# A new order for the beginning of a hybrid S5 / convolution trunk: inputs by quarters, the u projection one parameter group later, powers and copies moved between engines

## The chip, the cores and the metric

The kernel runs on one core of one Trainium2 chip. The metric is the device time of one execution in microseconds (us); the time before is the median of three executions, 2514.39 us (2512.59 to 2515.88).

## The reference

One inference step of two layers over a prompt of 1024 tokens and 8 sample tokens, d = 1024, in float32. Every layer is modulated by a shift, a scale and a gate that come from a conditioning vector (9 columns: one of the prompt, eight of the samples). Only the beginning matters here:

```python
mods = (silu(c) @ w_ada + b_ada).reshape(n, DEPTH, 2, 3, D)      # 96 blocks of 128 outputs
shift, scale, gate = mods[:, i, 0, 0], mods[:, i, 0, 1], mods[:, i, 0, 2]
h = x * (1.0 + scale) + shift
u = h @ w_in                                                     # then S5, 64 groups, 64 states
a_bar = exp(lam * dt); b_bar = ((a_bar - 1.0) / lam) * b
# states by a scan over time: s = a_bar * s + b_bar u;  y = re(c s) + d_skip * u
```

Behind it come the GLU of the S5 layer, a layer norm, a convolutional FFN, the short-convolution layer and a second FFN.

## The kernel before

Five engines run hand-written programs that meet at semaphores. Features lie on partitions: x is 8 chunks (k) of 128 features by 1032 tokens. A product in float32 is made of three float32r products: WH x HH, WH x HL, WL x HH, where HH and HL are the high and low half of the activations and WH and WL those of a weight unit (128 x 1024). `up_half` (L602) computes a part of one third (344 tokens) of one unit; a unit has three thirds of 8 x 3 matmuls.

**Loads.** One SyncE queue (L321) loads the conditioning vector, constants, then all eight first adaLN pairs (`FIRST`, 1 MB each; a pair is two of the 96 blocks), two raw units of w_in, the x chunks, and the other constants. Further adaLN pairs are loaded into the two slots of `ADA` from ScalarE's queue (`load_pair`, L1080), each when the pair two before has been multiplied (`take_partial`, L1085).

**First modulation.** TensorE multiplies the first eight pairs (L624), transposes their results (L632), Vector adds the bias (L1562), ScalarE modulates x chunk by chunk into a scratch tile (L1103), Vector makes HH by a cast and HL by a subtraction (L1566). The first product of u waits for all of it (`s_xfree`, L705), and for four more adaLN pairs.

**Eight groups.** For n = 0 to 7 TensorE computes one unit of u with three adaLN pairs between its parts (L707), then `s5_input(n)` (L645, transposes W2) and `s5_param(n)` (L654, the K0 products and the transposed B). Of a pair, `ada_partial` multiplies, ScalarE copies out, `ada_sum` adds the four partial sums, and ScalarE writes them to MOD (`take_mod`, L1092).

**Vector** computes the discretization (L1504 to L1538), the powers of a_bar in AP_ one by one (L1546), nine squarings of the unit angle factor, the last seven of them in UP7 (L1549 to L1557), eight copies into AR, the modulation above, then BB, and for each group `s5_params` (L1613): W2, the output constants CA, small copies into BD and CD, the rotation tables (which need the factor tables TA and TB16, `s_rtab`), and the K0 copy. Results go through SyncE to memory (L362) in one store of WT, CA, BD, CD, one of the rotation and one of K0.

**GpSimd** writes both halves of the weight units (`split_unit`, L452) and builds TA and TB16 by doubling (`factors`, L461; scratch in RB). It starts when the eighth first pair has been multiplied (L450), and the tables when `s_u7` says that the powers are ready.

Behind the last group follow the chunked scan (from `chunk_inputs(0)`, L820) and all later stages.

## Time and profile before

| | us |
|---|---|
| median of three executions | 2514.39 |
| the profiled execution | 2515.28 |
| its span in the profile | 2513.5 |
| TensorE busy | 2407.2 (96%) |
| VectorE busy | 1653.5 (66%) |
| ScalarE busy | 645.4 (26%) |
| GpSimd busy | 1015.3 (40%) |

The profile is of one execution. Times count from the start of its span. PE is TensorE's matmuls, PEld its weight loads, DVE VectorE, ACT ScalarE, POOL GpSimd, SP SyncE; a letter q behind an engine is its queue. L12 is line 12 of the kernel. In a timeline row stand start, duration, engine, line, instruction, output<-inputs with shapes and count, and in brackets how long the engine was idle before and what released it. Matmuls overlap, so their rate is read from the distance of their starts. The granted clock is a share of TensorE's full 2.4 GHz; 0.50 is 1.2 GHz.

### The profile page before, as it was taken

What the parts mean: (1) busy time and instruction counts of PE and PEld (TensorE: products, weight loads), DVE (VectorE), ACT (ScalarE), POOL (GpSimd) and SP (SyncE); (2) the same over time, 40 slices, a digit from 0 to 9 for tenths busy, and PEclk for the clock granted to TensorE, in tenths of its full rate; (3) what the DMA queues carried; (4) which work ended last, traced back from release to release, by engine and by line L of the source; (5) the groups of instructions that cost most, each with busy time, mean ns of one, the idle gap of its engine ahead of it and who ended that gap; (6) DMA issues with size and microseconds to landing.
All of it is one profiled execution on the core that took longest, in us unless ns stands there. A gap on an engine that the chain in (4) does not pass through costs nothing.

```text
span 2513.5 us, 39721 instructions
## 1 busy us (share of the span) xinstructions
PE 2407.2 (96%) x16080; PEld 2292.2 (91%) x16080; DVE 1653.5 (66%) x2230; ACT 645.4 (26%) x1273; POOL 1015.3 (40%) x505
## 2 busy tenths in 40 slices
PE   5898989999999999999999999999999999999996
PEld 2787789989999999999988999998999999999994
DVE  7888853367766666666774553575766676666675
ACT  1223421154212222222234101115222221221223
POOL 3322024347444434444325533434644443434430
PEclk8899999999999999999999999999999999999997
DMA  8686941111111111111101111110111111111102
GB/s 311 245 300 220 323 169 59 43 34 43 51 51 43 43 43 51 51 51 43 51 26 48 59 51 43 51 34 26 59 51 43 51 43 51 43 51 44 43 25 76
DMA packets 78112, 197.18 MB, mean 78 GB/s; under 512 B 27264, under 2 KB 34944, under 8 KB 76928
## 3 DMA queue, kind: packets, MB, share of 16 engines
q1 hardware_dynamic: 60992, 152.03, 17.7%
q10 hardware_dynamic: 16960, 42.80, 4.8%
q8 instruction: 127, 2.08, 0.3%
q14 instruction: 33, 0.27, 0.0%
HBM read 175.57 MB, written 19.23 MB: 78 GB/s over the span
## 4 chain that ended last, share of the span: by engine, by line
PE 81%; DVE 8%; ACT 4%; DVEq 3%; DMA 2%; issue 2%; SPq 0%; ACTq 0%
PE bank L609 17%; PE bank L611 17%; PE bank L610 17%; PE bank L886 8%; PE bank L888 7%; PE bank L887 7%; PE bank L589 1%; DVEq L2006 1%; PE bank L875 1%; PE bank L877 1%; PE bank L876 1%; DVE ROWS L2004 1%; PE bank L928 1%; ACT HH L1288 1%; ACT XRAW L1278 1%
## 5 line engine op out<-in xcount | busy, mean ns | idle before, releaser
L455 POOL TENSOR_TENSOR WH<-RAW,ZERO 128x1024 fp32r<-128x1024 f32 x188 | 389.9, 2074 | 1327.8 <-PE bank L611 632.9
L609 PE MATMUL bank<-HH,WH 128*128 128x344 f32 x2856 | 919.8, 322 | 1.1 <-ACT MOD L1097 0.7
L610 PE MATMUL bank<-HL,WH 128*128 128x344 f32 x2856 | 913.1, 320 | 0.0
L611 PE MATMUL bank<-HH,WL 128*128 128x344 f32 x2856 | 913.0, 320 | 0.0
L609 PEld LDWEIGHTS bank<-HH,WH 128*128 128x128 f32 x2856 | 537.2, 188 | 11.4 <-issue 11.4
L611 PEld LDWEIGHTS bank<-HH,WL 128*128 128x128 f32 x2856 | 537.5, 188 | 0.0
L610 PEld LDWEIGHTS bank<-HL,WH 128*128 128x128 f32 x2856 | 537.4, 188 | 0.0
L457 POOL TENSOR_TENSOR WL<-RAW,WH 128x1024 fp32r<-128x1024 f32 x188 | 530.6, 2822 | 14.7
L1847 DVE SCALAR_TENSOR_TENSOR X<-bank,MOD,X 128x344 f32<-128x344 f32 (+1 forms) x480 | 273.8, 571 | 325.6 <-PE bank L888 241.3
L886 PE MATMUL bank<-GH,WH 128*128 128x344 f32 x1248 | 408.3, 327 | 10.6 <-DVE X L1871 8.1
L888 PE MATMUL bank<-GH,WL 128*128 128x344 f32 x1248 | 399.6, 320 | 0.0
L887 PE MATMUL bank<-GL,WH 128*128 128x344 f32 x1248 | 399.4, 320 | 0.0
L886 PEld LDWEIGHTS bank<-GH,WH 128*128 128x128 f32 x1248 | 234.1, 188 | 30.4 <-DVE X L1871 11.0
L887 PEld LDWEIGHTS bank<-GL,WH 128*128 128x128 f32 x1248 | 234.8, 188 | 0.9
L888 PEld LDWEIGHTS bank<-GH,WL 128*128 128x128 f32 x1248 | 234.5, 188 | 0.0
L2004 DVE SCALAR_TENSOR_TENSOR ROWS<-ROWS,CWF 128x1024 f32<-128x1024 f32 x84 | 186.2, 2217 | 53.3 <-ACT ROWS L1346 53.3
L1367 ACT ACTIVATE ROWS<-ROWS 128x1032 f32<-128x1032 f32 x42 | 44.9, 1070 | 637.7 <-DVE ROWS L2010 637.7
L1346 ACT ACTIVATE ROWS<-bank,CWF 128x344 f32<-128x344 f32 x252 | 167.9, 666 | 0.0
L1342 ACT ACTIVATE ROWS<-bank 128x344 f32<-128x344 f32 (+1 forms) x252 | 119.1, 473 | 121.5 <-PE bank L611 108.1
L875 PE MATMUL bank<-HH,WH 128*128 128x344 f32 x384 | 129.0, 336 | 14.4 <-issue 11.5
L2009 DVE SCALAR_TENSOR_TENSOR ROWS<-STF,CWF,ROWS 128x8 f32<-128x8 f32 x84 | 131.1, 1561 | 13.6 <-issue 12.3
L2005 DVE SCALAR_TENSOR_TENSOR ROWS<-STF,CWF,ROWS 128x8 f32<-128x8 f32 x84 | 130.7, 1555 | 0.0
(329 smaller groups left out, 2434.6 us busy)
## 6 DMA issues: line engine op xcount, KB each, us to landing
RAW<-in_wstream SPq DMA_DIRECT2D x188, 512.0 KB, 3.2
ADA<-in_wada ACTq DMA_DIRECT2D x40, 1024.0 KB, 6.0
s_pack<-PKA SPq DMA_DIRECT2D x7, 1344.0 KB, 6.3
PKA<-s_pack SPq DMA_DIRECT2D x10, 512.0 KB, 6.8
XRAW<-in_xT SPq DMA_DIRECT2D x8, 516.0 KB, 16.5
X<-in_xT SPq DMA_DIRECT2D x1, 4128.0 KB, 12.3
PKA<-s_pack SPq DMA_DIRECT2D x7, 576.0 KB, 5.0
...
```

The source lines that it names most:

```text
L455: pool.tensor_tensor(WH[:, slot, :], RAW[:, slot % 2, :], bc(ZERO[:, :], [128, 1024]), ALU.add).then_inc(s_hi, 1)
L457: pool.tensor_tensor(WL[:, slot, :], RAW[:, slot % 2, :], WH[:, slot, :].bitcast(F32), ALU.subtract)\
L609: pe.matmul(o, wh, hh, start=k == 0, stop=False)
L610: pe.matmul(o, wh, hl, start=False, stop=False)
L611: m = pe.matmul(o, wl, hh, start=False, stop=k == KC - 1)
L875: pe.matmul(o, wh, hh, start=k == 0, stop=False)
L886: pe.matmul(out, wh, gh, start=q == 0, stop=False)
L887: pe.matmul(out, wh, gl, start=False, stop=False)
L888: m = pe.matmul(out, wl, gh, start=False, stop=q == 1)
L1346: act.activation(Tr[:, TH * t:TH * (t + 1)], b[:, 0:TH], ACT.Identity, bias=cwr[:, bass.ds(row, 1), 3:4].rearrange("p a b -> p (a b)"), sc ...
L1847: stt(xo, b[:, 0:w], MOD[:, gsec + o, 0:1], xo, M, A).then_inc(s_dev, 1)
L2004: stt(Tr[:, 0:SEQ], Ur[:, 1:1 + SEQ], cw[1], Tr[:, 0:SEQ], M, A)
```

## The change

The first loads are reordered: for each of four quarters p a shift pair, its scale pair, two x chunks, and for p < 2 a raw unit; then constants, and the first two pairs of `ADA` from SyncE's queue. The first pairs are multiplied with the packed form that the later pairs already use (`first_partial`, `first_sum`), ScalarE writes their modulations, then HH directly and the modulated chunk in place; Vector only subtracts (`chunks_low`). `first_u(p)` computes a quarter of the contraction (two chunks) of units 0 and 1 into six banks. The groups then hold units 2 to 7: group 0 has no u, and the others `U_STEP` thirds and `P_STEP` pairs each, pairs alternating between banks 4 and 5, thirds going through banks 0 to 3. Before, 4 later pairs stood ahead of u and 24 in the groups; now all 28 stand in the groups. The powers of a_bar are computed by doubling (three products of 32, 64 and 128 columns). The nine angle squarings and the modulation of the samples (`samples`, five small operations with four drains) are GpSimd's. ScalarE writes the high halves of units 0 to 9 (`hi_unit`) and the copies into BD and CD; GpSimd writes their low halves (`low_unit`, as `split_unit` without its first operation). Vector's group is split: W2 of group j, K0 of group j - 1, rotation j (rotation 0 only in group 1), output constants of group j. The store of a group is split in two, and `s5_param` now waits also for `s_ca`, the output constants.

```diff
+U_STEP = (0, 3, 3, 2, 2, 3, 2, 3)
+P_STEP = (2, 3, 3, 4, 4, 3, 5, 4)
+U_BANK = (0, 1, 2, 3, 0, 1, 2, 3, 0, 1, 2, 3, 0, 1, 2, 0, 1, 0)
+U_FREE = (0, 0, 0, 0, 1, 2, 3, 4, 5, 6, 7, 8, 9, 10, 11, 13, 14, 16)
+HI_AFTER = {1: 4, 2: 5, 3: 6, 5: 7, 6: 8}
...
-for i in range(8):
-    sp.dma_start(FIRST[i], wada[2 * i:2 * i + 2, :, :].rearrange("a p n -> p a n")).then_inc(s_first[i], 16)
-for n in range(2):
-    sp.dma_start(RAW[:, n, :], wstream[S_ORD[n], :, :]).then_inc(s_raw[n], 16)
-for k in range(KC):
-    sp.dma_start(XRAW[:, k, :], xT[:, k, :]).then_inc(s_xin[k], 16)
+for p in range(4):
+    for f, u in ((2 * p, 2 * p), (2 * p + 1, 8 + 2 * p)):
+        sp.dma_start(FIRST[f], wada[u:u + 2, :, :].rearrange("a p n -> p a n")).then_inc(s_first[f], 16)
+    for k in range(2 * p, 2 * p + 2):
+        sp.dma_start(XRAW[:, k, :], xT[:, k, :]).then_inc(s_xin[k], 16)
+    if p == 2:
+        for i in range(2):
+            sp.dma_start(BR[:, i], bT[i]).then_inc(s_br, 16)
+    if p < 2:
+        sp.dma_start(RAW[:, p, :], wstream[S_ORD[p], :, :]).then_inc(s_raw[p], 16)
...
+sp.wait_ge(s_fprod, 2)
+for a in range(2):
+    sp.dma_start(ADA[:, a], wada[ADA0 + 2 * a:ADA0 + 2 * a + 2, :, :].rearrange("a p n -> p a n"))\
+        .then_inc(s_adain[a], 16)
...
+def store_outputs(j):
+    sp.wait_ge(s_bdtev, j + 1)
+    sp.wait_ge(s_ca, j + 1)
+    sp.wait_ge(s_cd, j + 1)
+    sp.dma_start(pack_dram[j, :, PK_CA:PK_ROT], PKA[:, PK_CA:PK_ROT]).then_inc(s_pkc, 16)
+def store_k0(j):
     sp.wait_ge(s_kr, j + 1)
     sp.dma_start(k0_dram[j], KR).then_inc(s_krd, 16)
+for j in range(KC):
+    if j:
+        store_outputs(j - 1)
+        store_k0(j - 1)
     if j < KC - 1:
         sp.wait_ge(s_wtev, 2 * (j + 1))
-        sp.wait_ge(s_bdtev, j + 1)
-        sp.wait_ge(s_bd, j + 1)
-        sp.dma_start(pack_dram[j, :, 0:PK_ROT], PKA[:, 0:PK_ROT]).then_inc(s_pk, 16)
+        sp.dma_start(pack_dram[j, :, 0:PK_CA], PKA[:, 0:PK_CA]).then_inc(s_pkw, 16)
+        for i in ((), (0, 1))[j] if j < 2 else (j,):
+            sp.wait_ge(s_rot6, i + 1)
+            sp.dma_start(pack_dram[i, :, PK_ROT:PK], RB[i % 2]).then_inc(s_pkr[i % 2], 16)
     if j < 6:
         load_unit(j + 4, j % 2, S_ORD[j + 4] - j - 4 if j < 4 else 0)
-sp.wait_ge(s_pk, 16 * (KC - 1))
+store_k0(KC - 1)
+sp.wait_ge(s_pkw, 16 * (KC - 1))
+sp.wait_ge(s_pkc, 16 * (KC - 1))
 for i in range(2):
     sp.wait_ge(s_pkr[i], 64 - 16 * i)
...
+def angle_power(i):
+    z = [RB[1][:, 512 + NP_ * k:512 + NP_ * (k + 1)] for k in range(4)]
...
+    up = lambda lv: (UP7[:, 0, lv, :], UP7[:, 1, lv, :])
+    src = (Q[:, 17, :], Q[:, 18, :]) if i == 0 else z[2 * i - 2:2 * i] if i < 3 else up(i - 3)
+    product(z[2 * i:2 * i + 2] if i < 2 else up(i - 2), src, src, v)
...
-for n in range(2):
-    split_unit(n, n)
+for p in range(2):
+    low_unit(p, p)
+    samples(p)
+pool.wait_ge(s_fprod, 4)
 pool.wait_ge(s_u7, 1)
+for i in range(9):
+    if i == 4:
+        samples(2)
+    angle_power(i)
+samples(3)
+for n in range(2, 4):
+    low_unit(n, n % 2)
 factors(TB16, 0, 4)
 factors(TA, 4, 3).then_inc(s_rtab, 1)
-for n in range(2, U_S5):
-    pool.wait_ge(s_up, 3 * (n - 1))
-    split_unit(n, n % 2)
-pool.wait_ge(s_up, 3 * (U_S5 - 1))
-split_unit(U_S5, 0)
+for n in range(4, U_S5):
+    low_unit(n, n % 2)
+low_unit(U_S5, 0)
 pool.wait_ge(s_rot6, KC)
 pool.wait_ge(s_bdt, KC)
 pool.memset(TT[:, :, :], 0.0).then_inc(s_ones, 1)
 pool.wait_ge(s_krd, 16 * KC)
...
+def first_u(p):
+    pe.wait_ge(s_xfree, 2 * (p + 1))
+    for n in range(2):
+        pe.wait_ge(s_unit, n + 1)
+        for t in range(3):
+            if t == 2:
+                pe.wait_ge(s_xsmp, p + 1)
+            m = up_half(n, t, 2 * p, 2 * p + 2)
+            if p == 3:
+                m.then_inc(s_up, 1)
+pe.wait_ge(s_silu, 2)
+for p in range(4):
+    first_partial(2 * p)
+    first_partial(2 * p + 1)
+    if p == 0:
+        pe.wait_ge(s_cst, 16 * N_CST)
+    first_sum(2 * p)
+    first_sum(2 * p + 1)
+    if p > 1:
+        first_u(p - 2)
+first_u(2)
+first_u(3)
 pe.wait_ge(s_ones, 1)
...
+def pair(a):
+    if a:
+        ada_sum(a - 1, BK[4 + (a - 1) % 2][:, 256:274])
+    if a > 1:
+        pe.wait_ge(s_mod, a - 1)
+    ada_partial(a, BK[4 + a % 2][:, 0:256])
...
+    end = a + P_STEP[n]
+    if not U_STEP[n]:
+        pair(a)
+        a += 1
+        s5_input(n)
+    for i in range(U_STEP[n]):
+        if i == 1:
+            pe.wait_ge(s_kr, n)
+            pe.wait_ge(s_bdtev, n)
+            s5_input(n)
+            if n == KC - 1:
+                to_tokens(0)
+        pe.wait_ge(s_unit, 2 + m // 3 + 1)
+        if m > 3:
+            pe.wait_ge(s_ev, 6 + U_FREE[m])
+        third_of_u(m, 0, 4)
+        pair(a)
+        third_of_u(m, 4, 8).then_inc(s_up, 1)
+        m, a = m + 1, a + 1
     if n == KC - 1:
         to_chunks(0)
-    up_half(slot, 2, 2, 6)
-    ada_sum(a + 2, BK[6][:, 0:18])
-    if n == KC - 1:
-        pe.wait_ge(s_mod, a + 3)
-        s5_input(n)
-    up_half(slot, 2, 6, 8).then_inc(s_up, 1)
-    if n < KC - 1:
-        pe.wait_ge(s_mod, a + 3)
-        s5_input(n)
+    while a < end:
+        pair(a)
+        a += 1
     s5_param(n)
+ada_sum(a - 1, BK[4 + (a - 1) % 2][:, 256:274])
...
+def hi_unit(n):
+    slot = n % 2
+    if n > 1:
+        act.wait_ge(s_up, 3 * (n - 1))
+    act.wait_ge(s_raw[slot], 8 * (n - slot) + 16)
+    act.activation(WH[:, slot, :], RAW[:, slot, :], ACT.Copy).then_inc(s_hi, 1)
...
+        act.activation(LC[:, 0, k:k + 1], BK[7][:, 256 + 9 * i:257 + 9 * i], ACT.Identity, bias=LC[:, 1, k:k + 1])
...
+    for k in range(2 * p, 2 * p + 2):
+        act.wait_ge(s_xin[k], 16)
+        xk = XRAW[:, k, 0:SEQ]
+        act.activation(HH[:, k, 0:SEQ], xk, ACT.Identity, bias=MOD[:, k, 0:1], scale=LC[:, 0, k:k + 1])
+        act.activation(xk, xk, ACT.Identity, bias=MOD[:, k, 0:1], scale=LC[:, 0, k:k + 1]).then_inc(s_hx, 1)
+    if p < 2:
+        hi_unit(p)
...
+def take_bd(j):
     act.wait_ge(s_bdt, j + 1)
     act.activation(PKA[:, PK_BD:PK_BD + 256], BK[7][:, 0:256], ACT.Copy).then_inc(s_bdtev, 1)
...
+def b_diagonal(j):
+    if j:
+        act.wait_ge(s_k0, j)
...
+        for pl in range(2):
+            m = act.activation(BD[rows, pl, :, g2, :], BB[rows, pl, 4 * j:4 * j + 4, :], ACT.Copy)
+    m.then_inc(s_bd, 1)
...
+for n in range(2):
+    for t in range(3):
+        take_third(n, t)
+    hi_unit(2 + n)
...
+        take_bd(n - 1)
+    b_diagonal(n)
+    if not U_STEP[n]:
+        take_pair(a)
+        a += 1
+        take_input(n)
+    for i in range(U_STEP[n]):
+        if i == 1:
+            take_input(n)
+            if n == KC - 1:
+                act.wait_ge(s_pkr[1], 48)
+                take_tokens(0)
+        take_pair(a)
+        take_third(2 + m // 3, m % 3)
+        m, a = m + 1, a + 1
+    if n == KC - 1:
+        act.wait_ge(s_pkr[0], 64)
+        take_chunks(0)
+    sample_outputs(n)
+    while a < end:
+        take_pair(a)
+        a += 1
+    if n in HI_AFTER:
+        hi_unit(HI_AFTER[n])
+take_bd(KC - 1)
+take_mod(a - 1, BK[4 + (a - 1) % 2][:, 256:274])
+hi_unit(U_S5 + 1)
...
+def chunks_low(p):
+    for k in range(2 * p, 2 * p + 2):
+        dve.wait_ge(s_hx, k + 1)
+        tt(HL[:, k, 0:SEQ], XRAW[:, k, 0:SEQ], HH[:, k, 0:SEQ].bitcast(F32), S_).then_inc(s_xfree, 1)
...
-for k in range(2, KPH):
-    cmul((ap(0, k), ap(1, k)), (ap(0, k - 1), ap(1, k - 1)), (ap(0, 1), ap(1, 1)), tmp4)
...
+chunks_low(0)
+for m in (1, 2, 4):
...
+    cmul([AP_[:, pl, :, m + 1:2 * m + 1] for pl in range(2)],
+         [AP_[:, pl, :, 1:m + 1] for pl in range(2)], base, w)
+chunks_low(1)
...
 for k in range(L):
-    m = dve.tensor_copy(AR[:, :, :, L - 1 - k], AP_[:, :, :, k])
-m.then_inc(s_u7, 1)
...
 for j in range(KC):
-    s5_params(j, j == 0)
+    s5_input(j)
+    if j:
+        s5_kernel(j - 1)
+        if j == 1:
+            s5_rotation(0)
+        s5_rotation(j)
+    s5_outputs(j)
+s5_kernel(KC - 1)
```

## Rows read from the trace of the kernel before

**Rows 1.** The page's first part: busy microseconds and share of each engine.

```profile
PE 2407.2 (96%) x16080; PEld 2292.2 (91%) x16080; DVE 1653.5 (66%) x2230; ACT 645.4 (26%) x1273; POOL 1015.3 (40%) x505
```

**Rows 2.** Windows: length, busy us (count) by engine, clock, DMA share, GB/s.

```profile
10.00:40.00 30.00, 29.79 (x142) 12.68 (x140) 23.88 (x158) 2.35 (x4) 1.22 (x1) 1.00 1.03 408
72.00:97.00 25.00, 22.83 (x172) 19.18 (x172) 23.39 (x45) 5.59 (x17) 8.64 (x11) 0.88 0.46 167
97.00:230.10 133.10, 128.66 (x1110) 108.50 (x1110) 108.47 (x199) 37.93 (x108) 27.57 (x12) 0.99 0.81 294
98.00:100.00 2.00, 1.48 (x16) 0.69 (x16) 1.83 (x6) 0.00 (x0) 0.00 (x0) 0.58 0.55 217
114.26:132.86 18.60, 18.20 (x160) 15.39 (x158) 16.17 (x30) 5.18 (x15) 5.29 (x2) 1.00 0.84 301
47.57:76.20 28.63, 14.74 (x91) 9.27 (x92) 22.82 (x37) 12.47 (x20) 26.51 (x46) 0.50 0.68 239
```

**Rows 3.** TensorE's timeline: start, duration, instruction, idle before and releaser.

```profile
8.91 3.57 PE L627 MATMUL bank<-ADA,SC 128*9 128x256 f32 x8 [8.91 <-DMA ADA<-in_wada]
...
56.00 1.93 PE L589 MATMUL bank<-ADA,SCP 128*32 128x256 f32 x16 [16.21 <-DMA ADA<-in_wada]
58.95 0.99 PE L598 MATMUL bank<-STK,EVA 128*128 128x9 f32 x4 [1.01 <-ACT EVA L1090]
...
73.06 0.62 PE L609 MATMUL bank<-HH,WH 128*128 128x344 f32 x1 [0.71 <-ACT MOD L1097]
...
102.04 0.32 PE L609 MATMUL bank<-HH,WH 128*128 128x344 f32 x1
102.20 0.32 PE L610 MATMUL bank<-HL,WH 128*128 128x344 f32 x1
...
114.26 1.03 PE L650 MATMUL bank<-IDN,BR 128*128 128x128 f32 x8
115.70 0.67 PE L660 MATMUL bank<-PKA,BD 128*32 128x128 f32 x16 [0.40 <-ACT PKA L1163]
...
116.49 0.40 PE L609 MATMUL bank<-HH,WH 128*128 128x344 f32 x1
...
229.77 0.44 PE L666 MATMUL bank<-IDN,BD 128*128 128x128 f32 x2
```

**Rows 4.** Vector's timeline, 38 to 106 us.

```profile
38.64 8.87 DVE L1559 COPY AR<-AP_ 128x64 f32<-128x64 f32 x8
...
92.33 2.23 DVE L1671 TENSOR_TENSOR TP<-AW 128x512 f32<-128x512 f32 x1
...
98.51 0.69 DVE L1621 TENSOR_TENSOR TP<-AR,BB 128x512 f32<-128x512 f32 x1
...
102.01 0.69 DVE L1629 TENSOR_TENSOR BR<-TP 128x512 f32<-128x512 f32 x1
105.34 0.76 DVE L1640 TENSOR_TENSOR TP<-AP_,CR 128x576 f32<-128x576 f32 x1 [2.64 <-DMA s_pack<-PKA]
```

**Rows 5.** ScalarE's timeline at the first modulation.

```profile
49.02 2.37 ACT L1107 ACTIVATE UALL<-XRAW,MOD,LC 128x1024 f32<-128x1024 f32 x2 [9.69 <-issue]
```

**Rows 6.** GpSimd's timeline, 40 to 76 us.

```profile
40.82 2.34 POOL L457 TENSOR_TENSOR WL<-RAW,WH 128x1024 fp32r<-128x1024 f32 x1
...
47.93 0.26 POOL L470 TENSOR_TENSOR AW<-AW,UP 128x32 f32<-128x32 f32 x1
...
49.60 0.31 POOL L470 TENSOR_TENSOR AW<-AW,UP 128x64 f32<-128x64 f32 x1
...
63.98 0.62 POOL L473 TENSOR_TENSOR AW<-AW,UP 128x256 f32<-128x256 f32 x1
...
75.29 0.91 POOL L476 TENSOR_TENSOR AW<-AW 128x128 f32<-128x128 f32 x1
```

**Rows 7.** Instructions on tile ADA, 0 to 230 us: its loads' time to landing.

```profile
DMA to landing us min/median/max: 4.7/5.6/10.0
```

More of the change, by code:

```diff
@@ L52 @@
 NG = (96 - ADA0) // 2
-G_X, G_U = 4, 3
+G_U = sum(P_STEP)
 G_SCAN = (2, 2, 2, 2, 2, 1, 1)
@@ new lines, in first_sum @@
+            def first_sum(f):
+                pe.wait_ge(s_fev, f + 1)
+                for i in range(2):
+                    m = pe.matmul(BK[6 + f % 2][:, 256 + 9 * i:256 + 9 * (i + 1)], EVA[:, f % 2, 128 * i:128 * (i + 1)],
+                                  STK[:, :], start=True, stop=True, skip_group_check=True)
+                m.then_inc(s_ftr, 1)
+            def first_u(p):
[8 more added lines that the diff above has]
+                            m.then_inc(s_up, 1)
@@ new lines, in pair, with third_of_u @@
+            def pair(a):
[4 more added lines that the diff above has]
+                ada_partial(a, BK[4 + a % 2][:, 0:256])
+            def third_of_u(m, k0, k1):
+                n, t = 2 + m // 3, m % 3
+                o = BK[U_BANK[m]][:, 0:TH]
+                for k in range(k0, k1):
+                    wh = WH[:, n % 2, 128 * k:128 * (k + 1)]
+                    wl = WL[:, n % 2, 128 * k:128 * (k + 1)]
+                    hh, hl = HH[:, k, TH * t:TH * (t + 1)], HL[:, k, TH * t:TH * (t + 1)]
+                    pe.matmul(o, wh, hh, start=k == 0, stop=False)
+                    pe.matmul(o, wh, hl, start=False, stop=False)
+                    last = pe.matmul(o, wl, hh, start=False, stop=k == KC - 1)
+                return last
@@ new lines, in b_diagonal, with sample_outputs @@
+            def b_diagonal(j):
+                if j:
+                    act.wait_ge(s_k0, j)
+                else:
+                    act.wait_ge(s_pw, 1)
+                for g2 in range(2):
+                    rows = slice(64 * g2, 64 * (g2 + 1))
+                    for pl in range(2):
+                        m = act.activation(BD[rows, pl, :, g2, :], BB[rows, pl, 4 * j:4 * j + 4, :], ACT.Copy)
+                m.then_inc(s_bd, 1)
+            def sample_outputs(j):
+                if j:
+                    act.wait_ge(s_pkc, 16 * j)
+                else:
+                    act.wait_ge(s_cst2, 16 * N_CST2)
+                CD = PKA[:, PK_CD:PK_CD + 256].rearrange("p (x a b c) -> p x a b c", x=2, a=4, b=2)
+                for g2 in range(2):
+                    rows = slice(64 * g2, 64 * (g2 + 1))
+                    for pl in range(2):
+                        m = act.activation(CD[rows, pl, :, g2, :], CR[rows, pl, 4 * j:4 * j + 4, :], ACT.Copy,
+                                           scale=float(1 - 2 * pl))
+                m.then_inc(s_cd, 1)
@@ L1618, in s5_params @@
                 fence()
-                if not first:
+                if j:
                     dve.wait_ge(s_wt, 2 * j)
@@ L1635, in s5_params @@
                 fence()
-                if not first:
-                    dve.wait_ge(s_pk, 16 * j)
-                    dve.wait_ge(s_k0, j)
+                if j:
+                    dve.wait_ge(s_pkc, 16 * j)
                     dve.wait_ge(s_bdt, j)
@@ L1674, in s5_params, with s5_kernel @@
                 tt(R[:, 1], t[0], t[1], A).then_inc(s_rot6, 1)
+            def s5_kernel(j):
                 dve.wait_ge(s_k0, j + 1)
-                if not first:
+                if j:
                     dve.wait_ge(s_krd, 16 * j)
```

287 lines of the change are left out of this document (122 added, 165 removed).

## The prediction, made before the changed kernel ran

> **What bounds the kernel now.** I read the page first, then the windows of the beginning, then the timelines engine by engine. TensorE is busy 96% of the span [rows 1], so only its holes or its work can give time. The change touches nothing behind the point where the last parameter group is done, 230.1 us into the span (the last of [rows 3]); from there on both kernels run the same code on the same waits, so I forecast that point and move the rest of the span with it.
>
> Up to there three stages. First, 10 to 40 us: the queue moves 408 GB/s at a DMA share of 1.03 [rows 2]; it is full, and everything needed waits for it: the 8 MB of the first eight adaLN pairs are loaded before x. The first pair is there at 8.9 us [rows 3]. Second, 40 to 73 us: TensorE hardly works. Its next pair is waited for until 56.0 us, four pairs follow one by one, and the first product of u starts at 73.1 us [rows 3]. Vector's chain of powers and copies stands ahead of the modulation (the eight copies into AR alone end at 47.5 us) [rows 4]. Third, 73 to 230 us: eight groups, each one unit of u (3 thirds of 24 matmuls), three adaLN pairs and one S5 parameter group. One takes 18.60 us, of which TensorE is busy 18.20, at a clock of 1.00 and a DMA share of 0.84 (301 GB/s) [rows 2]. Here TensorE bounds, and Vector with 16.17 us follows closely.
>
> **Prices.** A matmul of 344 columns starts 0.157 us after the one before it (102.04 and 102.20 in [rows 3]), a third of u is 3.8 us. Transposes and products of one S5 group take 114.26 to 116.49 = 2.2 us, 0.4 of it a wait [rows 3]. So a pair with its sum and its restarts costs (18.6 - 72 x 0.157 - 2.2)/3 = 1.7 us. On Vector, W2 of one group is 98.51 to 102.70 = 4.2 us, the output constants are six operations of 0.76 us with the same two fences, 4.6 us [rows 4]; the rotation has six of W2's size, 4.2 us; with the K0 copies 0.5 us, a group is 13.5 us. On ScalarE a modulation of one x chunk is 1.2 us [rows 5]. On GpSimd a low half is 2.34 us; a complex product of 32 columns takes 47.93 to 49.60 = 1.67 us, its multiply of 256 columns 0.62 us undisturbed [rows 6]. The levels of the two factor tables are then 1.7, 2.0, 2.6, 3.9 and 1.7, 2.0, 2.6 us (the middle ones interpolated), with memsets about 17.5 us; in this trace they took 47.6 to 76.2 us, 28.6, while Vector was busy 22.8 us beside them [rows 2, 6].
>
> **Part 1, a new order of loads and u in quarters.** Pairs arrive as shift, scale, two x chunks, a raw unit. Counting megabytes behind the first landing at 0.41 MB/us: the scale pairs land at 11.5, 20.4, 29.4 and 38.4 us, the last x chunk at 41. From a landed pair to its modulation is partial 1.9, copy, sum 1.0, scalar copies (56.0 to 59.9 in [rows 3]), about 4.5 us at half clock. ScalarE then works 4 x 1.2 = 4.8 us for two chunks (high half and the chunk itself), where before Vector cast; the four quarters are ready at about 20, 30, 39 and, because the first quarter of u stands ahead of the last pairs on TensorE, not 47 but 51 us. Vector subtracts (1.2 us each). A quarter of the first two units is 36 matmuls, 5.7 us at full clock, about 8 at first (after the 2.6 us hole before 98.5 the clock granted was 0.58 in 98 to 100 us [rows 2]). Laid end to end: 33.5 to 41.5, two pairs, 45 to 62 us for three quarters. So two units are done at 62 us, where before the second ended at 114. Removed from the path: 23 us of waiting with TensorE idle or at 1.2 GHz.
>
> **Part 2, angle powers and samples to GpSimd.** Nine products of 1.67 us = 15 us and three of the four sample steps (five small operations and four drains, by the same row 2 us each) stand behind the second low half, which ends at 33.5 us: 54.5 us undisturbed. Vector works beside most of it, in operations of 0.7 to 1.2 us, so I take 60. The last samples are needed at 58.4, so TensorE loses 2 us. Less than nothing it can't cost, since the modulation never waited for these samples alone; the other end is rival (c). Low halves 2 and 3 wait for ScalarE, which waits for units 0 and 1: 68 us. Then the tables: 17.5 undisturbed, 28.6 as before; Vector has little to do after 70 us, so I take 19.5: 88 us.
>
> **Part 3, a new wait.** Vector does not ask for the tables in group 0 any more, but in group 1, ahead of the output constants of group 1. From 70 to 88 us it stands still. Then rotations 0 and 1 and the constants: 4.2 + 4.2 + 4.6 = 13.0 us, 101 us. Low half 4 will hold a Vector operation as now (a multiply of 0.69 us took 2.23 [rows 4]); this is inside my rounding of 3 us. TensorE, from 64, has group 0 (two pairs, no u) and group 1 (three thirds, three pairs), 5 + 17.5 us, is through at 86 and waits some 14 us for the constants of group 1. The eight small copies into BD and CD leave Vector for ScalarE, 1 us a group; ScalarE is busy 5.2 of 18.6 us [rows 2], so this costs and gains nothing.
>
> **Part 4, six groups from 101 us on.** 15 thirds, 23 pairs, 6 S5 groups without the 0.4 wait, tokens and chunks 2.1: 15 x 3.8 + 23 x 1.6 (one restart fewer, since sum and partial now stand together) + 6 x 1.8 + 2.1 = 107 us. Added: half clock after the wait, 2.5. Pairs with no u beside them: the load of a pair goes out when the pair two before is done, and takes 5.6 us to land [rows 7], so the second such pair waits 2.5 us and the group with three of them 3.3; with the copy between partial and sum in such a place (0.6 us at this clock), three groups, 8 us. High half 6 on ScalarE waits for a third that TensorE computes only in the next group; behind it on ScalarE are the copy of the transposed B, the next pair's copy and its load: 2 us at the B copy, 1 for the load behind it. Vector with 13.5 us a group and one hold of 1.5 stays inside the 17 to 20 of TensorE. Sum 107 + 2.5 + 8 + 3 = 120. By bytes: 23 pairs of 1.05 MB, six sets of stores of 1.97 and four raw units of 0.52 are 38 MB, at 301/0.84 = 358 GB/s 106 us, so the queue is close behind, but not the bound. So the last group ends at 101 + 120 = 221, say 220 us against 230.1: **10 us less**. The profiled execution took 2515.3 us with a span of 2513.5; it stood 0.9 above the median 2514.4. 2515.3 - 10 = 2505.3; against the median 2504.4; I say 2505.
>
> **Rivals.** (a) *The shared work hardly collides and loads keep up*: tables at 82 us, constants at 95, six groups in 109 us: 204, gain 26 us, 2489. For it: the six groups' matmuls fill only 107 us. Against: the DMA share of 0.84 at an 18.6 us group. (b) *The gain is given back at the ceilings*: DMA at 1.0 delays each pair by another microsecond, and the tables come at 92: constants at 106, 124 us behind them: 230, no change, 2515. For it: 28.6 us for tables of 17.5. (c) *Slower*: GpSimd and Vector run one after another. From 33.5 us on Vector has at most 28 us of work before the samples end; if all of it stands ahead of GpSimd's 21 us, the last samples are there at 83, two units at 87, low halves 92, tables 110, constants 123, groups 120: 243, 13 us slower, 2528. It decides from where the tables are later than 103 us. Against it: in 47.6 to 76.2 us Vector was busy 22.8 us [rows 2] and GpSimd, with 17.5 us of its own, ended 12 us earlier than the sum of both. The Trainium skill ("SBUF — State Buffer", Who interferes with whom) states this as a rule: a Vector instruction with two SBUF inputs and a GpSimd instruction that reads SBUF exclude each other for a whole instruction, and the loser blocks. By that rule in full, (c) would be the forecast, 2528. The trace agrees with holds of single instructions (0.69 became 2.23), not with full serial running. (d) *The change does not do what it says*: a quarter is held by another engine, so u starts late; with the first two units at 75 instead of 62 the tables and all behind move 13 us: (b)'s time or up to 2518.
>
> **Chances.** Forecast with its near surroundings (2498 to 2509) 0.50, (a) 0.20, (b) and (d) 0.20, (c) 0.10. For 8 in 10 the range leaves out (c) and the far end of (a): 2489 to 2516. About 0.2% (5 us) is what a measurement can tell from no change; so faster 0.70, same 0.20, slower 0.10. The likeliest case is faster, 2498 to 2509.
>
> **What would show it.** Units 0 and 1 done near 62 us (ScalarE's sixth copy of u); modulated x chunks in pairs 9 us apart; nine complex products on GpSimd between 34 and 60 us; the tables' end at 88 us; a wait of TensorE of 14 us for Vector's constants of group 1, with half clock behind it; then groups of 16 to 22 us with waits of 2 to 3 us for adaLN loads where no u is beside them, and a DMA share near 0.95; everything behind the last group shifted by one constant. I am wrong if GpSimd ends the tables outside 82 to 100 us, if Vector rather than TensorE sets the six groups, or if the stages after them do not shift alike.

## The result, and the profile of the changed kernel

The changed kernel takes 2527.28 us (median of 5 executions, 2524.47 to 2530.45), the kernel before 2514.64 on the same chip (5 executions, 2512.59 to 2516.0): a ratio of 1.005 with the interval 1.0036 to 1.0065. It is **slower by 12.6 us**; the forecast of 2505 was wrong in size and sign. The profile is of an execution of 2530.45 us, 3.2 above the median.

First the page: its busy times, which answer to [rows 1]. The work has hardly changed, the span has.

```profile
span 2528.7 us, 39804 instructions
PE 2398.7 (95%) x16096; PEld 2300.8 (91%) x16096; DVE 1616.9 (64%) x2075; ACT 680.9 (27%) x1383; POOL 1014.0 (40%) x569
```

Then windows, which answer to [rows 2] (length, then busy us and count by engine, clock, DMA share, GB/s): two stretches of the front, the stretch of the new wait, and the groups 2, 4 and 6 of the plan, counted from 0. A group is counted from the end of one block's last transposes of B to the end of the next block's.

```profile
50.00:60.00 10.00, 7.19 (x31) 7.19 (x32) 8.01 (x11) 0.00 (x0) 8.77 (x20) 0.66 0.03 13
60.00:70.00 10.00, 5.44 (x22) 5.16 (x22) 0.00 (x0) 2.84 (x5) 4.83 (x20) 0.74 0.00 1
100.00:120.00 20.00, 8.52 (x65) 7.54 (x66) 18.66 (x27) 2.45 (x10) 2.52 (x1) 0.66 0.40 141
113.20:132.40 19.20, 19.20 (x161) 16.95 (x160) 15.24 (x26) 6.44 (x23) 0.00 (x0) 0.93 0.76 265
151.10:176.70 25.60, 18.34 (x156) 14.90 (x155) 12.77 (x21) 7.63 (x27) 2.38 (x1) 0.83 0.73 264
194.90:221.60 26.70, 19.78 (x175) 15.17 (x175) 14.94 (x22) 9.60 (x32) 2.37 (x1) 0.81 0.75 274
```

In 50 to 70 us the queue moves next to nothing (0.03, 0.00) and the clock is between its two levels: TensorE has holes in the very stretch that was to be its best. In the six groups together (113.20 to 242.60 us) the DMA share is 0.77, where the prediction expected near 0.95. Groups 4 and 6 take 25.6 and 26.7 us for 18.3 and 19.8 us of matmuls; group 2, with the same kind of work, takes 19.2.

TensorE's waits of over 1.2 us in 48 to 222 us, from its timeline (start, duration, instruction, idle before and releaser), which answer to [rows 3]; two more waits for pair loads, of 2.26 us at 88.22 and 2.08 us at 148.88, are left out:

```profile
52.81 0.65 PE L677 MATMUL bank<-HH,WH 128*128 128x344 f32 x1 [4.01 <-POOL HL L508]
65.65 0.66 PE L677 MATMUL bank<-HH,WH 128*128 128x344 f32 x1 [4.56 <-POOL HL L508]
...
111.48 1.10 PE L754 MATMUL bank<-PKA,BD 128*32 128x128 f32 x16 [13.25 <-issue]
...
159.10 1.06 PE L743 MATMUL bank<-IDN,BR 128*128 128x128 f32 x8 [1.46 <-issue]
173.24 1.94 PE L657 MATMUL bank<-ADA,SCP 128*32 128x256 f32 x16 [4.87 <-DMA ADA<-in_wada]
...
210.73 0.61 PE L666 MATMUL bank<-STK,EVA 128*128 128x9 f32 x4 [2.97 <-ACT EVA L1226]
214.38 1.93 PE L657 MATMUL bank<-ADA,SCP 128*32 128x256 f32 x16 [3.04 <-DMA ADA<-in_wada]
```

The first two are released by L508 on GpSimd, the low half of the eight sample columns. Each first matmul behind them lasts 0.65 us where one at full clock lasts 0.32: the engine comes back at 1.2 GHz. Units 0 and 1 are done at 72.4 us.

GpSimd's timeline there, which answers to [rows 6]:

```profile
39.07 0.26 POOL L518 TENSOR_TENSOR AW<-AW 128x32 f32<-128x32 f32 x1
39.47 1.30 POOL L512 TENSOR_TENSOR AW<-AW 128x32 f32<-128x32 f32 x1
40.73 1.22 POOL L513 TENSOR_TENSOR AW<-AW 128x32 f32<-128x32 f32 x1
...
52.27 0.48 POOL L508 TENSOR_TENSOR HL<-CB,HH 128x16 fp32r<-128x16 f32 x1
...
65.37 0.22 POOL L508 TENSOR_TENSOR HL<-CB,HH 128x16 fp32r<-128x16 f32 x1
69.38 2.37 POOL L490 TENSOR_TENSOR WL<-RAW,WH 128x1024 fp32r<-128x1024 f32 x1 [3.79 <-ACT WH L1185]
74.00 2.36 POOL L490 TENSOR_TENSOR WL<-RAW,WH 128x1024 fp32r<-128x1024 f32 x1 [2.24 <-ACT WH L1185]
76.30 0.15 POOL L532 MEMSET AW<- 128x32 f32 x1
...
95.42 0.46 POOL L518 TENSOR_TENSOR AW<-AW 128x128 f32<-128x128 f32 x1
```

The samples of quarter 2 end at 52.75, behind four angle powers, and those of quarter 3 at 65.59, behind all nine: TensorE starts again at 52.81 and 65.65. GpSimd then waits for ScalarE's copies, which wait for TensorE. The tables take 76.30 to 95.88 = 19.6 us. The 13.25 us of TensorE at 111.48 are the wait for the constants of the second group, which Vector can only begin behind tables and rotations (Vector idles 15.00 us up to 95.98 for `AW L518`).

The two long groups on ScalarE and SyncE's queue:

```profile
157.67 1.06 ACT L1185 ACTIVATE WH<-RAW 128x1024 fp32r<-128x1024 f32 x1 [6.86 <-PE bank L816]
157.70 0.37 ACTq L1218 DMA_DIRECT2D ADA<-in_wada  x1
158.63 0.37 ACT L1271 ACTIVATE PKA<-bank 128x256 f32<-128x256 f32 x1
...
198.73 0.33 SPq L354 DMA_DIRECT2D RAW<-in_wstream  x1
199.18 0.35 SPq L380 DMA_DIRECT2D s_pack<-PKA  x1
...
209.14 0.26 ACT L1301 ACTIVATE PKA<-CR 64x64 f32<-64x64 f32 x1 [2.23 <-DMA s_pack<-PKA]
```

In group 4 the high half of unit 6 (L1185, which waits for TensorE's third, `bank L816`) stands ahead of the copy of the transposed B (L1271), without which TensorE doesn't go on at 159.10. In group 6 the stores of block 5 (199.18) stand in SyncE's queue behind the load of unit 9 (198.73), which waits until GpSimd has done unit 7; ScalarE at L1301 and TensorE at 210.73 wait for these stores.

Behind the groups the shift is not constant. The last transposes end at 242.58, 12.4 us later than before (230.2, the last of [rows 3]; the prediction has 230.1), but the spans differ by 15.2 us. The K0 store behind them is issued at once and its readers start 4.4 us later, against 1.6 in the kernel before; two pair loads, issued at 237.49 and 241.80 by ScalarE's queue, are in front of it. The difference arises there: the products of L861, which wait for constants that the same queue reads back behind those readers, start at 255.86, 14.6 us later than before (241.22), after a wait of 7.41 us for 3.81; the transposes at 272.98 are 15.0 us late (257.96).

### The profile page after: what moved, and what is told of

Read it like the earlier page. It is cut to its first block, busy times and chain, and to the rows that moved or that the text cites. A ratio compares the mean times of both kernels' runs of the same rounds, so it can differ in the third digit from the quotient of the medians.

```text
span 2528.7 us, 39804 instructions
## 1 busy us (share of the span) xinstructions
PE 2398.7 (95%) x16096; PEld 2300.8 (91%) x16096; DVE 1616.9 (64%) x2075; ACT 680.9 (27%) x1383; POOL 1014.0 (40%) x569
## 3 DMA queue, kind: packets, MB, share of 16 engines
q8 instruction: 127, 2.08, 0.3%
## 4 chain that ended last, share of the span: by engine, by line
PE 80%; DVE 7%; ACT 3%; DVEq 3%; DMA 3%; issue 2%; POOL 1%; SPq 1%; POOLq 0%; ACTq 0%
PE bank L677 16%; PE bank L679 15%; PE bank L678 15%; PE bank L990 8%; PE bank L992 7%; PE bank L991 7%; DMA ADA<-in_wada 1%; PE bank L979 1%; DVEq L2174 1%; PE bank L981 1%; PE bank L980 1%; PE bank L657 1%; PE bank L814 1%; DVE ROWS L2172 1%; PE bank L815 1%
## 5 line engine op out<-in xcount | busy, mean ns | idle before, releaser
L677 PE MATMUL bank<-HH,WH 128*128 128x344 f32 x2712 | 870.1, 321 | 8.6 <-POOL HL L508 8.6
L678 PE MATMUL bank<-HL,WH 128*128 128x344 f32 x2712 | 868.4, 320 | 0.0
L679 PE MATMUL bank<-HH,WL 128*128 128x344 f32 x2712 | 868.2, 320 | 0.0
L480 POOL TENSOR_TENSOR WH<-RAW,ZERO 128x1024 fp32r<-128x1024 f32 x178 | 367.7, 2066 | 1196.2 <-PE bank L679 533.1
L677 PEld LDWEIGHTS bank<-HH,WH 128*128 128x128 f32 x2712 | 511.3, 189 | 9.1 <-POOL HL L508 9.1
L679 PEld LDWEIGHTS bank<-HH,WL 128*128 128x128 f32 x2712 | 511.6, 189 | 0.0
L482 POOL TENSOR_TENSOR WL<-RAW,WH 128x1024 fp32r<-128x1024 f32 x178 | 505.9, 2842 | 13.9
L678 PEld LDWEIGHTS bank<-HL,WH 128*128 128x128 f32 x2712 | 511.2, 188 | 0.0
L979 PE MATMUL bank<-HH,WH 128*128 128x344 f32 x384 | 129.9, 338 | 14.0 <-issue 11.5
## 6 DMA issues: line engine op xcount, KB each, us to landing
XRAW<-in_xT SPq DMA_DIRECT2D x8, 516.0 KB, 15.6
X<-in_xT SPq DMA_DIRECT2D x1, 4128.0 KB, 12.2
UALL<-in_wada SPq DMA_DIRECT2D x4, 1024.0 KB, 17.7
```

Source lines behind the costliest of these rows:

```text
L480: pool.tensor_tensor(WH[:, slot, :], RAW[:, slot % 2, :], bc(ZERO[:, :], [128, 1024]), ALU.add).then_inc(s_hi, 1)
L482: pool.tensor_tensor(WL[:, slot, :], RAW[:, slot % 2, :], WH[:, slot, :].bitcast(F32), ALU.subtract)\
L677: pe.matmul(o, wh, hh, start=k == 0, stop=False)
L678: pe.matmul(o, wh, hl, start=False, stop=False)
L679: m = pe.matmul(o, wl, hh, start=False, stop=k == KC - 1)
L979: pe.matmul(o, wh, hh, start=k == 0, stop=False)
```

## The experiments

Three theories came out of this. **A**: the order on GpSimd makes the front late. **D**: two order blocks lengthen groups 4 and 6; its rival **E**: the pair loads do. **B**: Vector and GpSimd slow each other, and the order has no weight, the near relation of the prediction's rival (c). A ratio is always to the kernel before on the same chip, with its 95% interval. Differences between two changed kernels are differences of medians; some were taken on different chips, where the kernel before had 2514.6, 2513.6, 2514.1 and 2512.8 us, so an error of 1 to 2 us must be allowed them. Ends of groups are from one profiled execution each. "Last group" is the end of the last transposes of B (230.2 before, 242.6 in the changed kernel), "tables" the end of the second table (95.9), "second group" the end of its transposes (113.2).

### The samples ahead of the powers

```diff
             for i in range(9):
-                if i == 4:
+                if i == 0:
                     samples(2)
+                if i == 4:
+                    samples(3)
                 angle_power(i)
-            samples(3)
```

> GpSimd takes the samples of unit 2 ahead of the first angle power and those of unit 3 ahead of the fifth, instead of behind the fourth and the ninth. Theory A (the order on GpSimd): TensorE loses its two waits for HL (4.01 us at 52.81 and 4.56 us at 65.65) and the stretches at 1.2 GHz behind them, so the high and low halves of units 0 and 1 are done at 60 to 62 us instead of 72. The powers still end at about 65.6, so the low halves of units 2 and 3 can follow at once and not at 69.4 and 74.0; the tables end at 89 to 91 instead of 95.9, the second rotation's constants at about 105 instead of 111.3, the time is 2520 to 2523. Theory B (Vector and GpSimd slow each other, and the order is of no weight): the tables keep their end near 96 whatever the samples' place, and the time stays at 2526 to 2529. Theory C (the whole loss lies in the group loop): the front may come earlier, but the groups stretch by as much, and the time stays at 2526 to 2529.

2520.63 us, 1.0037 (1.0023 to 1.0051): 6.6 us under the changed kernel. Windows of this kernel:

```profile
50.00:60.00 10.00, 10.00 (x65) 10.00 (x64) 8.81 (x12) 3.19 (x6) 8.63 (x19) 1.00 0.04 14
60.00:70.00 10.00, 5.16 (x67) 3.34 (x66) 4.48 (x8) 6.02 (x21) 9.09 (x20) 1.00 0.67 247
```

TensorE is busy 10.00 of 10 us at a clock of 1.00 where it had 7.19 at 0.66, and the queue, idle in 60 to 70 us before, is at 0.67. Tables 89.3, second group 106.5, last group 233.7. Theory A holds, as forecast here: units 0 and 1 are done at 60.3 us, and the six groups take 127.2 us for 129.4, so they don't stretch. B's and C's times did not come. The interval of the ratio still overlaps the changed kernel's (1.0036 to 1.0065), so it is the profile that shows the gain, not the time alone.

### The powers back on Vector

```diff
 # Vector, behind RHO
+            nine squarings of (q(17), q(18)) into UP7, then s_u7
 # GpSimd
-            wait s_u7; powers 0 to 3; samples(2); powers 4 to 8; samples(3)
+            samples(2); samples(3)
             for n in range(2, 4):
                 low_unit(n, n % 2)
+            pool.wait_ge(s_u7, 1)
             factors(TB16, 0, 4)
```

> The nine angle powers go back to Vector, between RHO and the AR copies; GpSimd does samples 2 and 3 at once, then the low halves of units 2 and 3, and then waits for the powers before the tables. Theory A (the order on GpSimd is what is late): units 0 and 1 are done on TensorE at 60 to 64, the tables end at about 87, the constants of the second rotation at about 102, and the time is 2517 to 2520, some 9 us under the changed kernel. Theory B (Vector and GpSimd slow each other): the same operations cost Vector more than the 10 to 12 us that they took off GpSimd, and the tables end at 92 or later, the time is 2523 or more. What is left over 2514.6 after this is the group loop's.

2523.03 us, 1.0031 (1.0018 to 1.0043). The tables end at 88.5 as expected, but the time is above the expected 2517 to 2520, in the range that was named for theory B, whose other signs (tables at 92 or later, the operations dearer on Vector) did not come. Two rows of this kernel, GpSimd and Vector:

```profile
61.21 2.56 POOL L490 TENSOR_TENSOR WL<-RAW,WH 128x1024 fp32r<-128x1024 f32 x1 [17.37 <-ACT WH L1182]
...
61.46 2.93 DVE L1806 TENSOR_TENSOR TP<-AP_,CR 128x576 f32<-128x576 f32 x1
64.46 2.77 DVE L1808 TENSOR_TENSOR PKA<-TP 128x576 f32<-128x576 f32 x1
```

On Vector the 54 operations take 35.12 to 43.90 = 8.8 us, where GpSimd needed 24. But GpSimd then stands idle for 17.37 us ahead of 61.21, with the powers ready at 44: the tables could have run there. A group loop left alone keeps its excess (last group 236.0, 130.4 us behind the second). Also, Vector's 0.76-us operations beside the low halves take 2.93 and 2.77.

### The high half of unit 6 one group later

```diff
-HI_AFTER = {1: 4, 2: 5, 3: 6, 5: 7, 6: 8}
+HI_AFTER = {1: 4, 2: 5, 4: 6, 5: 7, 6: 8}
```

> The high half of unit 6 is made in group 4 of the plan instead of group 3; nothing else moves. Theory D (an order block in the loop): in the changed kernel hi_unit(6) stands on ScalarE ahead of the copy of a pair's results that TensorE needs, and the fourth group took 25.5 us where its neighbours took 18.2 to 19. With the high half one group later that group takes 19 to 21 and the next gets at most 2 us longer; the last group ends at about 238 instead of 242.6 and the time is 2522 to 2524. Theory E (the group is long because adaLN pair loads come late, 4.87 us at 173.24): the group stays at 24 to 26 and the time at 2526 to 2529.

2521.88 us, 1.0030 (1.0012 to 1.0048). The group goes from 25.6 to 19.4 us, the next from 18.2 to 19.8, all six from 129.4 to 125.3; the last ends at 238.1. The copy that was held is that of the transposed B, not that of a pair's results. TensorE's wait for a pair load, and SyncE's queue, in this kernel:

```profile
167.83 1.93 PE L657 MATMUL bank<-ADA,SCP 128*32 128x256 f32 x16 [0.93 <-DMA ADA<-in_wada]
...
152.07 0.32 SPq L380 DMA_DIRECT2D s_pack<-PKA  x1
...
174.17 0.33 SPq L354 DMA_DIRECT2D RAW<-in_wstream  x1
```

The wait for a pair load falls from 4.87 to 0.93 us. SyncE's stores of the block wait for the same copy of B; in the changed kernel they went out at 159.02, in one bunch with the next stores and a raw unit (163.42), beside the pair load of 163.45, which took 9.8 us from its issue until TensorE could start (173.24); here they go out at 152.07, and the load of 162.00 takes 5.8. So the order block made the late load too: theory D for this group. The raw unit also goes out later here (174.17), and this run can't tell its share from that of the stores.

### Half of each later pair load

```diff
-                act.dma_start(ADA[:, a % 2], wada[ADA0 + 2 * a:ADA0 + 2 * a + 2, :, :]...)
+                act.dma_start(ADA[:, a % 2, 0], wada[ADA0 + 2 * a])
```

> Each later adaLN pair load brings only the first of its two blocks, so half of these bytes aren't moved; the values of the second block are left out of the computation (its buffer keeps what it had). Theory E (the pair loads bound the loop, as the queue is short of time there): the four waits of TensorE for ADA (12.2 us) go, with the half clock behind them; the groups from the second on take 18 to 19 each, the last ends at 230 or before, and the time is 2512 to 2518. The k0 store behind the last group lands 2 to 3 us sooner. Theory D (order blocks): the fourth and sixth group keep most of their excess of 7 us each, and the time falls by 3 to 5 us at most, to 2522 to 2525.

2513.93 us, 1.0002 (0.9993 to 1.0012). TensorE's waits in the first 280 us:

```profile
PE bank L754 <- issue: 16.6, 1, 16.6
PE bank L699 <- DMA ADA<-in_wada: 8.9, 2, 8.3
PE bank L677 <- POOL HL L508: 8.7, 2, 8.0
PE bank L861 <- DMA PKA<-s_pack: 5.8, 1, 5.8
...
PE bank L657 <- DMA ADA<-in_wada: 3.3, 3, 1.5
```

The waits of L657 were 12.2 us and are 3.3; the six groups take 118.1 us instead of 129.4, the last ends at 230.9, and the wait behind it (L861) is 5.8 instead of 9.9. The front is as late as in the changed kernel. So the loads' time is worth 11 us in the loop and some 2 behind it. Theory E's numbers came within 1 us, D's did not; but a load behind a bunch of stores is helped by half the bytes as well as by its stores going earlier, so this run doesn't refute D.

### A new order of the front

```diff
 # Vector: RHO; powers; chunks_low(2); AR and q; chunks_low(3); BB
 # GpSimd
+            samples(2)
+            samples(3)
             pool.wait_ge(s_u7, 1)
-            nine powers with the samples between and behind them
+            factors(TB16, 0, 4)
             for n in range(2, 4):
                 low_unit(n, n % 2)
-            factors(TB16, 0, 4)
             factors(TA, 4, 3).then_inc(s_rtab, 1)
```

> The angle powers on Vector directly behind RHO (54 operations that took 9.1 us there in the kernel a2), Vector's low halves 2 and 3 moved up behind them, and GpSimd in the order samples 2 and 3, first table, low halves of units 2 and 3, second table. In a2 GpSimd stood idle 17.37 us ahead of 61.21 although the powers were done at 44.0. The group loop is as in the changed kernel. Theory A (GpSimd's order sets the tables' end, and this sets TensorE's wait in the second group): tables done at 68 to 72 instead of 95.9, no wait of over 4 us of TensorE behind unit 2, the second transposes of BD at 88 to 92 instead of 113; the groups behind them become some us longer than 129 in all, because the loads have less time, the last ends at 222 to 228, the time is 2508 to 2513. Theory F (the group loop is bound by transfers, whatever its start): the last group ends where the loads let it, at 232 or later, and the time is 2516 or more. Theory B (Vector and GpSimd slow each other): the tables take 25 us or more beside Vector's BB and constants, but end by 76.

2511.7 us, 0.9998 (0.9987 to 1.0009): 15.6 us under the changed kernel, last group 222.9, both in the expected range; second group at 96.3 and tables at 81.8 are later than expected. The powers take 8.8 us on Vector, as above, not 9.1. GpSimd's table rows of this kernel:

```profile
48.26 0.16 POOL L532 MEMSET AW<- 128x32 f32 x1
...
65.72 1.24 POOL L518 TENSOR_TENSOR AW<-AW 128x256 f32<-128x256 f32 x1
67.16 5.42 POOL L490 TENSOR_TENSOR WL<-RAW,WH 128x1024 fp32r<-128x1024 f32 x2 [0.20 <-issue]
72.53 0.15 POOL L532 MEMSET AW<- 128x32 f32 x1
```

The first table takes 48.26 to 66.96 = 18.7 us beside a Vector that is busy 17.7 us of them; in the changed kernel, beside one that is busy 4.5 us, 76.3 to 89.3 = 13.0. So theory B is true as a price, 5.7 us on one table, and false as the cause: the tables still end 14 us sooner. Theory F falls too: the groups didn't stretch, they take 126.6 us.

### The load of unit 9 behind the stores

```diff
-                if j < 6:
+                if j < 5:
                     load_unit(j + 4, ...)
+                if j == 6:
+                    load_unit(9, 1)
```

> Only SyncE's load of unit 9 (which waits for the low half of unit 7) is moved from ahead of the stores of block 5 to behind those of block 6. Theory D (an order block): in the changed kernel the stores of block 5 were issued only at 199.18, ScalarE's and Vector's work on the next block stood behind them, and the sixth group took 26.7 us. Now it takes 20 to 23, the last ends at 237 to 239 instead of 242.6, and the time is 2521 to 2524. Rival: the pair loads alone bound that group (3.04 us of waiting at 214.38 and half clock): it stays at 25 or more and the time at 2526 to 2529.

2525.11 us, 1.0049 (1.0030 to 1.0067). The stores of block 5 go out at 194.24 instead of 199.18 and the 2.97 us for EVA are gone, but the group only falls from 26.7 to 24.7: a wait of 3.09 us for a pair load stays in it. The last group ends at 239.1, but 1.6 of these 3.5 us lie ahead of the second group (111.6 for 113.2), where nothing was changed. The block was real and cost 2 us, not 4 to 6; the interval holds the changed kernel's 1.005, so the time alone doesn't show it.

### Front and loop together, and even pairs

> The new front of b1_front, with the high half of unit 6 one group later (a3) and the load of unit 9 behind the stores of block 6 (b2). If the three causes are independent, the gains add: from b1_front some 5 us for the high half and 4 for the load come off, the last group ends at 214 to 219 and the time is 2499 to 2505, under the 2514 of the kernel before. Theory F (the queue bounds the loop: 28 pair loads, stores and units): the gains overlap, the last group ends at 222 or later, and the time is 2507 or more.

2504.22 us, 0.9962 (0.9951 to 0.9972), 9.9 us under the kernel before. The last group ends at 215.9, the last six take 120.0 us: 18.4, 19.4, 17.3, 18.6, 24.5 and 21.7. Group 6 has lost 2 us of its excess and keeps the rest, with a wait of 2.46 us for a pair load. TensorE and Vector in the front of this kernel:

```profile
73.02 1.10 PE L753 MATMUL bank<-PKA,BD 128*32 128x128 f32 x16 [7.08 <-issue]
94.92 0.67 PE L753 MATMUL bank<-PKA,BD 128*32 128x128 f32 x16 [2.44 <-issue]
...
67.21 2.89 DVE L1813 TENSOR_TENSOR TP<-AP_,CR 128x576 f32<-128x576 f32 x1
70.18 2.74 DVE L1816 SCALAR_TENSOR_TENSOR PKA<-TP 128x576 f32<-128x576 f32 x1
81.58 0.69 DVE L1829 TENSOR_TENSOR TP<-AW 128x512 f32<-128x512 f32 x1 [3.66 <-POOL AW L520]
```

The wait for the second group's constants is 2.44 us instead of 13.25; a wait of 7.08 for the first group's has come up, as in the kernel with the new front alone (7.40); its last operations stand beside GpSimd's low halves.

The next kernel adds `P_STEP = (2, 3, 3, 4, 4, 4, 4, 4)`:

> As b3_front_and_loop, and the later pairs are spread as 2, 3, 3, 4, 4, 4, 4, 4 over the groups instead of 2, 3, 3, 4, 4, 3, 5, 4. The group with five pairs had 3.04 us of waiting for a pair load and 2.97 for a partial sum. If even spreading matters: one waiting stretch at 1.2 GHz goes, 2 to 4 us under b3. If the queue is the bound: the same time as b3 within 1.5 us, since the bytes are the same.

2502.67 us, 0.9954 (0.9938 to 0.9971). The group of five pairs falls from 24.5 to 21.8 us, the one before it grows from 18.6 to 20.9; the intervals overlap, so the even spreading gives nothing that can be told. Its profiled execution has the last group 3.1 us later (219.0) at a median 1.6 us lower: so much for what one profile says of a whole span.

### The powers on GpSimd in the better order

```diff
 # against the front-and-loop kernel
+            powers on GpSimd: samples(2), four, samples(3), five
             factors(TB16, 0, 4); low_unit(2); low_unit(3); factors(TA, 4, 3)
```

> As b3_front_and_loop, but the angle powers stay on GpSimd as in the changed kernel; its order is samples 2, four powers, samples 3, five powers, first table, low halves 2 and 3, second table, and Vector's low halves stand where they stood in the changed kernel. This parts the order on GpSimd from the powers' engine. Theory A1 (order alone would have done): with the powers ending at about 65.5 and the low halves of units 2 and 3 (5.4 us) within the tables (19.6 us), the tables end at 90 to 92, 9 us behind b3, but TensorE has its low half of unit 2 only at about 82, so the second group is late by about 10 us, and the time is 2510 to 2515. Theory A2 (the front is hidden behind something else): tables as late, but the time within 3 us of b3's 2504.

2513.71 us, 1.0000 (0.9990 to 1.0009). Tables 89.3, second group 104.3, last group 225.5. TensorE of this kernel:

```profile
80.53 0.66 PE L817 MATMUL bank<-HH,WH 128*128 128x344 f32 x1 [14.09 <-POOL WL L492]
```

The wait has only another name here: with the low halves ahead of the tables (the first experiment) it was 16.4 us for the constants, and the second group was done 2 us later. Against the front-and-loop kernel the powers' engine, together with the place of Vector's low halves, is worth 9.5 us. With the powers on GpSimd, samples early and both loop blocks gone, the change as a whole gives nothing over the kernel before.

### Two finer trials

`P_STEP = (2, 3, 4, 4, 4, 4, 4, 3)`, against the kernel with even pairs:

> As b4_flat_pairs, but the later pairs are 2, 3, 4, 4, 4, 4, 4, 3 by group, so no pair stands behind the thirds of the last group. Theory G: the k0 store behind the last group (issue to landing 4.4 us in b4, 1.5 in the kernel before) stands behind pair loads issued just ahead of it; with them some 4 us earlier it lands in 1.5 to 2.5 us, the Toeplitz loads start 2 us sooner and the time is 2 to 3 us under b4's 2502.7. Rival: the wait of the first chunk inputs (7.9 us in b4) is set by the reading of the other constants, not by the k0 store, and the time stays within 1 us of b4; or the fourth pair in the third group costs as much there.

2504.24 us, 0.9963 (0.9950 to 0.9975). SyncE's queue of the kernel with even pairs, and of this one:

```profile
219.14 0.32 SPq L385 DMA_DIRECT2D s_k<-Q  x1
223.57 3.87 SPq L413 DMA_DIRECT2D TT<-s_k  x8
```

```profile
220.56 0.32 SPq L385 DMA_DIRECT2D s_k<-Q  x1
222.17 3.16 SPq L413 DMA_DIRECT2D TT<-s_k  x7
```

In the first, pair loads go out at 213.89 and 218.21; in the second, the last one ahead of the store goes out at 216.52. From store to readers 4.4 us become 1.6, as theory G says, and the wait of the first chunk inputs falls from 7.87 to 4.75. But in group 3 there is now a wait of 3.65 for a pair load, and the groups end 1.4 us later. The mechanism is shown, the gain was paid for elsewhere.

The low half of unit 3 behind the second table, also against even pairs:

> As b4_flat_pairs, but the low half of unit 3 stands behind the second table. In b3 the two low halves on GpSimd (66.88 to 72.3) held two of Vector's operations on the first constants for 2.89 and 2.74 us instead of 0.76, and TensorE waited 7.08 us for these constants. Theory B (Vector and GpSimd hold each other): with one low half there one hold goes, the first constants are done 2 us sooner and the tables end 2.5 us sooner, at 79; the time is 2 to 3 us under b4's 2502.7. Rival: the hold moves to another operation, and the time is within 1 us of b4.

2503.2 us, 0.9954 (0.9938 to 0.9971). Vector's held operations:

```profile
66.55 2.74 DVE L1812 TENSOR_TENSOR TP<-AP_,CR 128x576 f32<-128x576 f32 x1
79.76 2.88 DVE L1830 TENSOR_TENSOR TP<-AW 128x512 f32<-128x512 f32 x1
```

One hold is gone, the first constants are done two microseconds sooner (the wait is 3.89), the tables end at 79.0, and the hold comes back in a rotation; the second group ends at 96.4 as before. The rival was right.

## Why the prediction was wrong

By its own steps, up to the end of the last group, where 220 to 221 became 242.6:

- **Part 1 held.** The modulated quarters are there at 20.2, 29.6, 37.7 and 46.6 us for forecast 20, 30, 39 and 51. TensorE was at full clock (1.00 in 30 to 47 us), which fits the last one's coming sooner.
- **Part 2 failed, in one step: "TensorE loses 2 us".** It asked only when the last samples end, and never placed those of quarter 2, which it had counted in the same sum. Both were waited for, 4.01 and 4.56 us, each with a stretch at 1.2 GHz behind it; units 0 and 1 were done at 72.4 instead of 62. Behind this stands a mis-sized term, the price of a product beside a busy Vector: nine products took 36.2 to 63.7 less 3.3 for the samples, 24 us, where 15 was the undisturbed price and 20 the step's allowance. The first four took 13.1 us where 6.7 was undisturbed. With 26.5 us allowed for work of 21, quarter 2's samples would by the same count have ended at about 47 us; TensorE asked for them at 48.8 and got them at 52.75. Running the other way: the earlier the x chunks are ready, the longer TensorE waits for the samples. The first experiment takes both holes away and gives 6.6 us; taking the powers off GpSimd gives 9.5 more where the loop is repaired.
- **The tables' size was right, 19.6 for 19.5 us.** Their start was 8 us late (68 was forecast for the last low half, 76.3 it was), and so their end: 95.9 for 88. This is inside the 82 to 100 us that the prediction gave itself, so that sign stayed silent.
- **Part 3 held in kind.** TensorE's wait is 13.25 us for forecast 14, with both of its ends some 10 us late. From tables to constants it is 15.4 for 13.0 us: the hold by low half 4, 2.83 us instead of 0.69, was called rounding and isn't.
- **Part 4 failed in two groups.** The forecast gave 120 us from the constants on, and 131.3 passed. Of these 1.9 are the last products and transposes of group 1 behind its constants, which the sum of six groups leaves out. Split over the groups by its own terms, the sum gives groups 2, 3, 5 and 7 20.5, 18.2, 18.0 and 21.7 us (measured 19.2, 18.7, 18.2 and 21.0), and groups 4 and 6 21.2 and 20.7 (measured 25.6 and 26.7). The step on the high half of unit 6 had the mechanism and half of the price: it counted 2 + 1 us, and the run without it gives 6.2 in that group, 4.1 over all six. The load of unit 9 ahead of the stores, 2 us, wasn't in the prediction at all. The rest of group 6 goes with the pair loads: it takes 22.6 us with half of their bytes; with the load of unit 9 moved it takes 24.7, and 21.8 when the loop also has four pairs there instead of five. The mean DMA share of the six groups is 0.77, where the front has up to 1.05, so the queue as a whole isn't full; what delays the single loads stays open. With both blocks gone and the front repaired, six groups take 120.0 us. That this equals the forecast is luck: its 120 holds 3 us for the high half and 2.5 for half clock that this kernel doesn't pay, and group 6 is 3.8 us over.
- **"Everything behind shifted by one constant" was off** by 2.7 us, counted from the prediction's 230.1: the last pair loads delay a 64 KB store. From store to readers it is 4.4 us, 2.7 with halved pairs and 1.6 with earlier ones. This was the one of the prediction's signs of being wrong that came.

7.9 us at the tables, 2.4 at the constants, 11.3 in the groups and 2.7 behind them make 24.3, and 0.9 for rounding 221 to 220.1: 25.2, the distance of the span 2528.7 from the forecast's 2513.5 - 10. The medians are 22.9 apart (2527.3 and 2504.4); the other 2.3 are the profiled executions' distances from their medians.

Of the rivals, (c) named the time, 2528, by luck and not by the cause. It put the tables at 110 and its threshold at 103; they ended at 95.9, and the kernel was slower all the same, since nearly half of the miss lies in the loop. The rule of the Trainium skill ("SBUF — State Buffer", Who interferes with whom) came out in between: one low half holds one Vector operation for up to its own length (0.76 us become 2.93), and small operations of GpSimd grow from 0.26 to as much as 1.30; but 13.0 us of table took 18.7 beside a Vector that was busy 17.7 of them, far from one after the other. (d), a quarter held by another engine, had the mechanism of the front nearly right: two units at 75 (72.4 measured), and 13 us behind them (the tables were 7.9 late). It was given 0.20 together with (b), and its price was carried only to 2518, because the loop was taken at its forecast. As (d) was a question that the order of GpSimd's program answers without a chip, it should not have been a chance but a sum. The front repaired alone is worth 15.6 us and the two loop blocks 7.5 on top, 23.1 in all. That this is the size of the miss doesn't prove the list of causes: the repaired kernel has the powers back on Vector, so it is not the one that was forecast, and its constants of the second group are there at 94.9 us, 6 ahead of the forecast's 101. With the powers left on GpSimd the same repairs end at 2513.7, 9 us over the forecast.
